# Order of index page loads, weight loads and key copies around two stages of a hybrid decode step

## What is computed

```
layer 0: h = rms(x); A = differential attention (4 heads), B = gated linear recurrence (4 heads)
         A and B come from ONE projection h @ w_in_ab; x += concat(A, B) @ w_out_ab
layer 1: h = rms(x); C = sparse attention:
         iq, ik, iw = indexer parts of h @ w_in_c
         isc  = relu(iq . ik_all).sum over 8 heads, weighted by iw    # ik_all = cached index pages + new keys
         keys = top_k(isc, 256 for samples, 128 for the prompt);  grouped attention over these keys only
         x += C @ w_out_c
each layer then: x += cross_attention(rms(x), memory); x += gated_mlp_with_conv(rms(x)); at the end rms(x)
```

## Time and profile before

| | us |
|---|---|
| median of 3 runs | 2208.92 (2207.28 to 2212.73) |
| the profiled execution | 2212.33 |
| its span, first to last instruction | 2210.7 |
| PE busy | 2089.9 (95%) |
| DVE busy | 1227.5 (56%) |
| ACT busy | 708.2 (32%) |
| POOL busy | 272.7 (12%) |

### The profile page before, as it was taken

One profiled execution on the slowest core, in us unless ns is written; L12 is line 12 of the kernel. 1 busy time (PEld: TensorE's weight loads), 2 busy tenths in 40 slices (PEclk: granted clock), 3 DMA queues, 4 the chain that ended last, 5 costly groups with the idle time before them and its releaser, 6 DMA issues.

```text
span 2210.7 us, 37289 instructions
## 1 busy us (share of the span) xinstructions
PE 2089.9 (95%) x15230; PEld 1876.6 (85%) x15230; DVE 1227.5 (56%) x2035; ACT 708.2 (32%) x1085; POOL 272.7 (12%) x241
## 2 busy tenths in 40 slices
PE   8989899999999999999998999899998999999997
PEld 6756698789978999999996577669976999999996
DVE  4457367765343566436644799764443466525652
ACT  5234434433232322212233425443331322212222
POOL 0012002432000000000003235420000100000001
PEclk9999999999999999999999899999999999999998
DMA  5368323324452222222224125642343222222221
GB/s 192 118 232 272 109 79 122 115 81 134 157 186 86 77 82 86 77 86 77 82 79 129 41 78 193 203 124 96 127 166 123 77 84 80 86 77 87 77 80 53
DMA packets 221612, 249.26 MB, mean 113 GB/s; under 512 B 18578, under 2 KB 175644, under 8 KB 221238
## 3 DMA queue, kind: packets, MB, share of 16 engines
q1 hardware_dynamic: 199322, 196.35, 27.9%
q0 software_dynamic: 9872, 28.65, 4.0%
q10 hardware_dynamic: 12248, 21.88, 3.0%
HBM read 233.63 MB, written 13.00 MB: 112 GB/s over the span
## 4 chain that ended last, share of the span: by engine, by line
PE 84%; DVE 6%; ACT 3%; issue 2%; DMA 2%; SPq 1%; PEld 1%; POOL 0%; ACTq 0%; PEldq 0%; DVEq 0%; POOLq 0%
PE PS L839 54%; PE PS L817 10%; PE PS L899 5%; PE PS L1272 1%; PE PS L1287 1%; PE PS L1594 1%; PE PS L1575 1%; DMA C<-in_cache_diff_k 1%; PE PS L977 1%; DVE stat L2567 1%; DVE arena L2474 1%; PE PS L1305 1%; PE PS L1647 1%; PE PS L1150 1%; SPq L599 1%
## 5 line engine op out<-in xcount | busy, mean ns | idle before, releaser
L839 PE MATMUL PS<-xr_r,WH 128*128 128x288 f32 (+2 forms) x1920 | 569.8, 297 | 0.8 <-POOL W_r L672 0.8
L839 PE MATMUL PS<-hT_r,WH 128*128 128x288 f32 (+2 forms) x1856 | 550.9, 297 | 4.2 <-issue 2.3
L839 PE MATMUL PS<-hT_r,W_r 128*128 128x288 f32 (+2 forms) x1856 | 550.2, 296 | 0.0
L2424 DVE TENSOR_TENSOR W_r<-W,WH 128x1024 fp32r<-128x1024 f32 (+1 forms) x219 | 282.3, 1310 | 353.5 <-ACT WH L1736 353.0
L839 PE MATMUL PS<-arena_r,WH 128*128 128x224 f32 (+2 forms) x1920 | 437.4, 297 | 1.5 <-issue 1.5
L1736 ACT ACTIVATE WH<-W 128x1024 fp32r<-128x1024 f32 (+1 forms) x262 | 266.4, 1034 | 487.2 <-PE PS L839 310.4
L839 PEld LDWEIGHTS PS<-xr_r,WH 128*128 128x128 f32 x1920 | 362.6, 189 | 1.5 <-issue 1.5
L839 PEld LDWEIGHTS PS<-hT_r,WH 128*128 128x128 f32 x1856 | 350.3, 189 | 6.5 <-issue 6.5
L839 PEld LDWEIGHTS PS<-hT_r,W_r 128*128 128x128 f32 x1856 | 350.2, 189 | 0.0
L839 PEld LDWEIGHTS PS<-arena_r,WH 128*128 128x128 f32 x1920 | 324.2, 189 | 2.6 <-issue 2.5
L839 PE MATMUL PS<-arena_r,W_r 128*128 128x288 f32 (+2 forms) x704 | 208.7, 296 | 0.0
(11 more groups left out here) (438 smaller groups left out, 3046.3 us busy)
## 6 DMA issues: line engine op xcount, KB each, us to landing
W<-in_w_ffn_in SPq DMA_DIRECT2D x176, 256.0 KB, 3.3
W<-in_w_ffn_out SPq DMA_DIRECT2D x40, 512.0 KB, 3.4
W<-in_w_in_ab SPq DMA_DIRECT2D x28, 512.0 KB, 3.6
C<-in_cache_mem_k SPq DMA_DIRECT2D x10, 1024.0 KB, 8.4
C<-in_cache_diff_k POOLq DMA_DIRECT2D x32, 256.0 KB, 4.2
C<-in_cache_diff_k SPq DMA_DIRECT2D x32, 256.0 KB, 3.6
C<-in_cache_diff_v POOLq DMA_DIRECT2D x32, 256.0 KB, 4.9
C<-in_cache_diff_v SPq DMA_DIRECT2D x32, 256.0 KB, 4.7
```

The lines of the kernel that those rows point to most:

```text
L839: ins = mm(o, w[:, k, c * 128:c * 128 + 128], v(k0 + k)[:, t0:t1], start=opens and first and k == 0 and e == 0, stop=last and k == nk - 1 ...
L2424: v_.tensor_tensor(slot_view(WL, NW, n), slot_view(W, NW, n), plain(slot_view(WH, NV, n)), ALU.subtract).then_inc(lo_done, 1)
```

## The change

Three edits.

1. `LOADS` in front of `c_qkv`: the index pieces are woven with the five weight slots: piece 0, slot F+6, piece 1, slots F+7 and F+8, piece 2, slots F+9 and F+10, piece 3. Before it was pieces 0, 1, 2, slots F+6 to F+10, piece 3. `CL`, and with it POOL's order, is as it was.
2. `blocks` gets a flag `held`, used for `a_in` alone, on ACT and DVE. Before the last block it makes one slot less (12 rather than 13 is the last), and after the block it makes none. Slot 13 is made right after the copies of the first half of sample 0's keys. Slot 14 is left to `b_gates`' first `ahead`, after attention A.
3. The second half of sample 0's keys is copied by DVE and ACT in turn ("DADA"), not by DVE alone ("DDDD").

```diff
@@ LOADS @@
-        caches(lambda: CL.extend([("ik", p, 0) for p in range(NB // 2)]))
+        ik_first = len(CL)
+        CL.extend([("ik", p, 0) for p in range(NB // 2)])
+        for p, count in enumerate((1, 2, 2, 0)):
+            LOADS.append(("c", ik_first + p))
+            LOADS.extend([("w", n) for n in range(at, at + count)])
+            at += count
         rest("c_qkv", "xk1")
@@ tensor, after a_in @@
-            as_keys("DDDD")
+            as_keys("DADA")
@@ scalar and vector, both alike @@
-            def blocks(name, end=len(stream)):
+            def blocks(name, end=len(stream), held=False):
                 for b in ORDER[name]:
-                    ahead(min(S["slot"] + len(b) + 2, end))
+                    last = held and b is ORDER[name][-1]
+                    ahead(min(S["slot"] + len(b) + (1 if last else 2), end))
                     S["slot"] += len(b)
                     yield b
-                ahead(min(S["slot"] + 3, end))
+                if not held:
+                    ahead(min(S["slot"] + 3, end))
@@ scalar, copies @@
-                for b, ((a, z), _) in enumerate(zip(dst, blocks(name, end), strict=True)):
+                for b, ((a, z), _) in enumerate(zip(dst, blocks(name, end, name == "a_in"), strict=True)):
@@ scalar and vector, in a_in @@
                 if b == 2:
                     act.wait_ge(stores, 32)
                     as_keys("DADA", 0)
+                    ahead(S["slot"] + 2)
@@ scalar and vector, after a_in @@
-            as_keys("DDDD", 1)
+            as_keys("DADA", 1)
@@ vector, a_in @@
-            for b, _ in enumerate(blocks("a_in")):
+            for b, _ in enumerate(blocks("a_in", held=True)):
```

## The result

The changed kernel takes 2197.73 us (median of 5 runs, 2195.96 to 2199.99), the kernel before 2208.92: the ratio of the runs is 0.9944, 95% interval 0.9929 to 0.9959 (the quotient of the two medians is 0.9949). Three more sets of runs of it were taken beside the experiments, on two chips. All its 35 runs together have a mean of 2201.8 and all 82 of the kernel before beside them a mean of 2210.7: 8.9 us less, plus or minus 1.7. The first measurement was a good one; the effect to explain is 9 us rather than 11.

A forecast was written before the change was run, and what follows sets the result against it. PE bounds the kernel (84% of the chain), losing time in three pauses and the low clock behind them. Gains of 3.5 + 4.6 + 7.2 = 15.3 us off 2208.9 give 2194 us; range 2190 to 2203.

The forecast's parts named there:

- place A: Sample 0's keys, where PE idles 2.19 and 2.32 us while DVE makes slot parts before copying; 8.1 us gain predicted.
- A1: First half of sample 0's keys: 2.7 us less wait plus 0.8 us from the kept clock, 3.5 us in sum.
- A2: Second half of sample 0's keys: 2.8 us less wait plus 1.8 us of clock, 4.6; 2.1 if the clock falls.
- Slot 14 until after attention: After attention: making slot 14 there fits ACT's 4.2 us pause and costs nothing; 2.3 us were the cover gone.
- Attention lets the gain through: Inside attention: cached-key loads, SP, POOL and waits all move with PE, so the whole earlier gain passes.
- Rival 3: Attention: low-clock spells of 3.5 us at up to six stops make the kernel slower, +6, 2215 us; chance 0.05.
- The weave's wait: Indexer: ACT no longer waits for slot F+6, PE's second index pair starts at 1206.9, not 1210.85: 4.0 us.
- B: The indexer, with the woven loads: 4.0 us of wait plus 3.2 of clock, 7.2 us; 4.0 if the clock falls.
- The clock holds: Keys and indexer: PE about 60% busy, no pause over 1.5 us, so granted clock stays 1.00.
- the mixed case: Clock holds at the keys and falls at the indexer: 8.1 + 4.0 = 12.1 us, 2197 us; chance 0.15.
- Rival 1: Both places: pauses go but low clock stays, as transposes don't count as busy; 8.8 us, 2200 us; chance 0.15.
- Rival 2: Indexer: the weave frees nothing, ACT still waits or pages are late; only 8.1 us, 2201 us; chance 0.08.

The follow-up runs named there:

- e7: Changed kernel with the old load order and the second half of the keys copied by DVE alone; 2203.08 us, 9.1 less than the kernel before.
- e1: Changed kernel with the loads in the old order, so only the edits to the keys and slots 13 and 14; 2202.76 us, 7.3 less than the kernel before.
- after: First measurement and profile of the changed kernel with all three edits; 2197.73 us against 2208.92 before.
- e3: Kernel before with only the second half of the keys copied by DVE and ACT in turn; 2210.93 us, 0.0 less than the kernel before.
- e5: Changed kernel plus identity transposes as fillers in PE's short pauses around the indexer; 2196.66 us, 14.8 less than the kernel before; measured again 2197.37 us.
- e2: Kernel before with only the weave of index pages and weight slots; 2206.0 us, 3.7 less than the kernel before.
- e4: Kernel before plus 15 identity transposes in each of the two PE pauses at sample 0's keys; 2206.49 us, 4.4 less than the kernel before.

## Why the prediction was right, and where it wasn't

The time came out inside the range and 4 us above the forecast of 2194; over all 35 runs the gain is 8.9 us, where the sum said 15.3. So the direction and place A were understood, and the sum was not: 6.4 us of it did not come. Step by step:

*A1, the first half of the keys: right.* Predicted 2.7 of wait and 0.8 of clock; measured 2.6 and 0.7.

*A2, the second half: right in size, wrong in who does it.* Predicted 2.8 of wait and 1.8 of clock; measured 2.4 and 1.7. The last copy is ACT's, 0.60 us, as foreseen, but e7 shows that DVE alone would have done as well. Together A brings 7.5 us at DVE's first reduce (predicted 8.1). e1, the keys alone, gave 7.3, plus or minus 1.9.

*Slot 14 until after attention: free, as predicted.* In after and in e1 ACT makes its high part 2.4 us behind the start of slot 12, inside its wait for PE, and PE goes through slots 12 and 13 without a wait for the parts.

*Attention lets the gain through: right on the mean, with a noise I hadn't priced.* The "att" column runs from 123.8 to 131.5 us, and it does so in kernels in which nothing of attention differs: 130.5 before, 125.6 in e3, whose run time is that of before. The four profiles that don't hold slots back have a mean of 128.7, the nine that do 127.0: 1.7 us less, plus or minus 2.9, so no loss and no gain that these profiles can tell. The extra 4 us of the first pair of profiles lie within this spread; in the second profile of the same kernel slot 12 comes at 244.5, not 240.8. Read at slot 12, the gain of A is 3.7 us in the profile of e7 and 11.8 in that of e1, whose place A differs by 0.05 us. Rival 3, spells of low clock inside attention: there is such a spell in one profile of the changed kernel (0.66 in 122 to 127) and not in its other three; no kernel with A's edit lost by them, in the mean, what A had won. What makes attention's spread is open.

*The weave's wait: the mechanism was right, and it pays only if PE is on time.* Predicted 4.0 us; the two halves of the table give 38.7 against 42.5 when PE keeps its clock, 3.8 us, and nothing when it needs 41 us for its slots. The mean of ik1 over the seven profiles with the weave is 40.2, over the six without it 42.7: 2.5 us. For B as a whole the means are 84.8 and 87.6: 2.8 us.

*"The clock holds": the step that failed, at B.* I took PE at about 60% busy, with no pause over 1.5 us, to be safe, since the stretch of 128.9 to 138.0 was the earlier trace rows. Place A bore that out. At B three things were wrong with it. First, I looked only at the stretch behind the removed pause. The clock also falls ahead of it, behind the 20 matmuls of 2 columns and 1.01 us of idle at the mean by token, a place that was at 1.00 in the profile before and that I therefore took as fixed; it differs from one execution to the next. Without the weave such a spell costs little: in e1 the slots took 4.0 us longer than before and the second index pair came 0.3 us later. The weave takes that cover away, and the spell is paid in full. Second, the 3.2 us of clock behind the index pairs hardly came. PE still has pauses of 1.57, 0.73 and 0.96 us for DVE (I had said none over 1.5), and the stretch of 11 us has 0.78 or 0.79 in three profiles of the changed kernel and 0.84 in the fourth. The chain of before, and then that of after, show what became of it:

```profile
1221.93 4.85 PE PS L1485 x16
```

```profile
1210.17 4.85 PE PS L1490 x16
1215.02 3.84 PE PS L1502 x10
```

`prompt_index` starts 11.1 us behind the second index pair before and 9.8 after, so the first 1.3 us were won. But the low clock now falls on what comes next: the first `sample_index` takes 3.84 us, where it took 3.08 and I had counted on 2.05. From the second index pair to the next projection it takes 45.5 us before, and 45.3, 45.2, 45.3 and 44.2 in the four profiles after. The low spell was moved, not removed. Third, even in e5, which is at 1.00 up to 1204.3, it falls to 0.66 behind that, and this stretch takes 44.2. B as a whole was predicted at 7.2; in the four profiles of the changed kernel it brings 0.2, 4.1, 4.0 and 1.0 against the one profile before, and the e2 runs say 3.7. That profile is one of six without the weave, which run from 85.6 to 88.9.

*Sum.* A 7.5 and B between 0 and 4 give 7.5 to 11.5, and 8.9 was measured. The outcome is the mixed case, which I gave 0.15: the clock holds at A and falls at B, and that case was put at 12.1 us because it still let B have its 4.0 of wait in full. The first measurement made the forecast look better than it was, and that was luck: its mean of 2198.0 us lies 4.4 us under that of the 30 later runs of the same kernel, 2202.4, and the median of the second set, 2203.3, is just outside the range. Two sums of the prediction were also wrong. Four spells at 3.5 us are 14 us, which is all of A and most of B, not half of it. And the named cases with a gain above 6.6 us add up to a chance of 0.88, not 0.83. Neither touches the forecast.

*The rivals.* Rival 1, by the rule on transposes, would have the low clock stay in both places; the changed kernel at A, and e4, show it wrong there. At B the low clock did come in every profile of the changed kernel: its mean is 0.72 to 0.79 over the first 10.5 us behind the start of the second index pair. But in both profiles of e5, which adds nothing but transposes there, it is 1.00 over the same stretch, so the rule on transposes is not what lowers it. Rival 2, that ACT still waits for a weight load or the pages are late: no such wait in any of the seven profiles with the weave.

*What stays open.* Why the clock falls at the mean by token in one execution and not in the next. The Trainium skill (TensorE: Matmul & The Clock Gate, Part 1: The HAM clock gate) says that activity is judged in a window which runs free of the program. That would let the same instructions be judged in two ways; no run here moved the one against the other, so it is not shown.

## What to carry to other kernels

Ask of every wait that you remove what it was hiding: here it had absorbed low-clock spells of up to 4 us ahead of it, so the gain on paper was there in full only in the profiles without them. Where two engines prepare a buffer for later and a third stands idle for a copy, first move the preparation behind the copy; a second engine for the copies is worth testing by itself and may bring nothing. And before a difference of a few microseconds between two profiles is given to the change, look at the same stretch in a third profile, if possible of a kernel that doesn't touch it.

## What the runs showed of the hardware

- Idle transposes as fillers kept the granted clock at 1.00 through two waits of 2.2 and 2.3 us, after which it otherwise fell (0.69 in the mean of a window, and low in all three profiles with these waits idle). They returned 3.7 us in the one profile and 4.4, plus or minus 2.3, in the runs.
- Behind 2.16 us of matmuls with 2 columns and a pause of 1 us the clock was low for the next 3 to 7 us in five of ten profiles. It cost 1.5 to 2.7 us on 48 matmuls of 288 columns. With the pause filled by transposes it still fell in one profile of three, and cost 1.2 us.
- One SP issue of an index page takes 1.0 to 1.1 us, in a row of 24 or in groups of 8 (8.00, 7.95, 8.36 us); the weight loads woven between them cost 0.4 to 0.5 us each when their place is free.
- Runs of one kernel have a standard deviation of 1.5 to 6 us, so a few runs can't tell 4 us; the same stretch of attention varied by 7.7 us between profiles.
